# A decoder step in which VectorE turns the cached keys in 32x32 blocks, TensorE scores them by 32x32 block products, and the memory keys come first

## The reference, cut to what matters

```python
k_all = concatenate([pool_k[page_table].reshape(Bd, P, KV, 128), k_new], axis=1)   # cached pages, then the new key
s = einsum('bqkgd,blkd->bkgql', qg, k_all) * 128 ** -0.5                           # 8 samples x 12 heads x 2049
s = s + bias                     # layer 0: ALiBi and the mask of the chosen 256; layer 1: forgetting bias
p = softmax(s); o = einsum('bkgql,blkd->bqkgd', p, v_all)
sm = einsum('bqhd,bmhd->bhqm', qm, cache_mem_k) * 128 ** -0.5                       # 8 x 4 x 256 memory scores
```

## Time and profile before

| | before |
|---|---|
| time, three runs | 2242.54, 2244.25, 2245.08 us |
| profiled execution, first to last instruction | 2232.3 us |
| TensorE busy | 2170.8 us, 97% |
| VectorE busy | 661.5 us, 30% |
| ScalarE busy | 485.6 us, 22% |
| DMA, all queues | 647.34 MB, mean 290 GB/s |
| granted TensorE clock, mean | 0.990 |

### The profile page before, as it was taken

The page is one execution under the profiler, slowest core; times in us unless marked ns, Lnnn a source line. Parts: engine busy times, 40 slices in busy tenths (PEclk is TensorE's granted clock), DMA queues, the critical chain, the costliest instruction groups (busy, mean ns, idle before and its releaser), DMA issues.

```text
span 2232.3 us, 32324 instructions
## 1 busy us (share of the span) xinstructions
PE 2170.8 (97%) x12529; PEld 1346.5 (60%) x12529; DVE 661.5 (30%) x1225; ACT 485.6 (22%) x1106; POOL 4.3 (0%) x10
## 2 busy tenths in 40 slices
PE   8999999999999999999899999999999999999999
PEld 7778875678844435343488886645788444343534
DVE  0239961610662222212500010033115622222223
ACT  1221016520331001010310215643104211010112
POOL 0000000000000000000000000000000000000000
PEclk9999999999999999999999999999999999999999
DMA  9743548794359999999955457998642699999994
GB/s 274 233 149 115 198 152 259 214 344 150 114 228 425 420 429 413 428 420 422 380 164 161 144 188 245 356 348 305 243 145 107 248 426 425 427 427 429 424 428 192
DMA packets 213854, 647.34 MB, mean 290 GB/s; under 512 B 55400, under 2 KB 88953, under 8 KB 184161
## 3 DMA queue, kind: packets, MB, share of 16 engines
q1 hardware_dynamic: 180673, 637.39, 73.8%
q10 hardware_dynamic: 33056, 8.27, 1.9%
HBM read 639.62 MB, written 5.96 MB: 289 GB/s over the span
## 4 chain that ended last, share of the span: by engine, by line
PE 88%; DMA 9%; ACT 2%; DVE 1%; issue 1%; SPq 0%; ACTq 0%; DVEq 0%
PE bank L681 22%; PE bank L1379 14%; PE bank L1178 10%; PE bank L1426 9%; PE bank L1440 6%; DMA ring<-in_w_down 5%; PE bank L915 4%; DMA ring<-in_w_up 4%; PE bank L1352 4%; PE bank L925 2%; PE bank L1055 2%; PE bank L1036 1%; ACT arena L1528 1%; PE bank L1002 1%; PE bank L1262 1%; PE bank L970 1%
## 5 line engine op out<-in xcount | busy, mean ns | idle before, releaser
L1379 PE MATMUL bank<-ring,AT 128*64 128x512 f32 x2048 | 457.3, 596 | 11.5 <-DMA ring<-in_w_up 8.2
L1528 ACT ACTIVATE arena<-bank 128x512 f32<-128x512 f32 (+5 forms) x519 | 255.8, 540 | 811.5 <-PE bank L681 231.0
L681 PE MATMUL bank<-X,ring 128*128 128x264 f32 x1664 | 385.6, 389 | 6.2 <-ACT X L1778 6.2
L681 PEld LDWEIGHTS bank<-X,ring 128*128 128x128 f32 x1664 | 312.3, 191 | 64.2 <-issue 13.3
L1379 PEld LDWEIGHTS bank<-ring,AT 128*64 128x64 f32 x2048 | 142.4, 137 | 287.2 <-issue 272.4
L1426 PE MATMUL bank<-ring,arena 128*64 128x512 f32 x1024 | 224.3, 594 | 18.7 <-ACT arena L1528 13.8
L1178 PE MATMUL bank<-AT,ring 128*128 128x264 f32 x1024 | 232.6, 390 | 0.0
L2441 DVE TENSOR_TENSOR X<-bank,X 128x264 f32<-128x264 f32 x256 | 110.7, 432 | 361.6 <-PE bank L1440 359.6
L1178 PEld LDWEIGHTS bank<-AT,ring 128*128 128x128 f32 x1024 | 196.8, 193 | 34.1
L1426 PEld LDWEIGHTS bank<-ring,arena 128*64 128x64 f32 x1024 | 75.6, 137 | 157.2 <-issue 154.5
L1440 PE MATMUL bank<-arena 128*128 128x264 f32 x512 | 138.8, 402 | 0.0
(11 more groups left out here) (342 smaller groups left out, 1385.2 us busy)
## 6 DMA issues: line engine op xcount, KB each, us to landing
ring<-in_w_gate SPq DMA_DIRECT2D x64, 2048.0 KB, 16.8
ring<-in_w_up SPq DMA_DIRECT2D x48, 2048.0 KB, 15.5
ring<-in_w_down SPq DMA_DIRECT2D x48, 2048.0 KB, 12.9
ring<-in_w_o SPq DMA_DIRECT2D x16, 2048.0 KB, 12.1
ring<-in_w_up SPq DMA_DIRECT2D x32, 1024.0 KB, 7.6
ring<-in_w_down SPq DMA_DIRECT2D x32, 1024.0 KB, 15.8
ring<-in_cache_b_k SPq DMA_DIRECT2D x128, 256.0 KB, 4.3
ring<-in_cache_b_v SPq DMA_DIRECT2D x128, 256.0 KB, 4.8
```

The source lines that it names most:

```text
L681: mm = pe.matmul(B[4 * (g % 2) + f][:, 0:n_tok], u[:, c * 512 + f * P:c * 512 + (f + 1) * P], src[8 * half + c][:, 0:n_tok], start=(half = ...
L1379: mm = pe.matmul(B[bank][64 * s:64 * s + 64, :], M.xsT[:, at:at + 64], ring[slots[s][0]][:, c * FE:(c + 1) * FE], start=(half == 0 and c = ...
L1528: return act.activation(out, in_, ACT.Copy, scale=scale)
```

## The change

The cached keys are no longer turned by TensorE and copied by ScalarE. VectorE turns each `k` unit in place with one instruction (`turn_keys`), which transposes each 32x32 block by itself. Inside a block of 32 positions and 32 head numbers the numbers now lie along 32 partitions; the four blocks of positions of a page lie in the four partition quarters. So a product has 32 rows and 32 columns: `Qz` is built with each of the four quarters d of the query copied to all four partition quarters (`query_blocks` on TensorE, `pad_queries` on ScalarE), and partition quarter r writes its scores to bank r, summed over d and the key heads. In layer 0 a unit is now one sample with 16 pages and a product group holds 4 units; in layer 1 a unit is one sample with 8 pages and a group holds 2.

The memory units stand ahead of the cached units in the plan, in the scores and in the softmax; the four memory heads use four 32-column groups instead of two, in tiles of their own in `AT`. The new key's scores come from products on VectorE (`new_keys`) and one matmul. The spread mask is added by TensorE behind the last group (`cached_mask`), and `add_mask` is gone. The first half of `prompt_topk` stands behind the turning of the keys, the second half in the middle of the softmax of the cached scores.

```diff
-    u += [("k", k, 128 // n) for k in range(n)] + [("mk", k, 4) for k in range(2)]
+    u += [("mk", k, 4) for k in range(2)] + [("k", k, 128 // n) for k in range(n)]
...
+        def key_unit(layer, u):
+            if layer == 0:
+                return u, 0, PAGES
+            return 2 * (u // 4) + u % 2, 8 * (u // 2 % 2), PAGES // 2
...
+            def query_blocks(a, x):
+                if x == 4:
+                    pe.wait_ge(S("slab_copied"), cnt["slab"] - 1)
...
+                    for d in range(4):
+                        for r in range(4):
+                            mm = pe.matmul(B[4][32 * r:32 * r + 32, 96 * d:96 * d + 96], ident[:, 32 * d:32 * d + 32], new,
+                                           start=True, stop=True)
...
-                slab(layer, "mkv", 0, Ac, SEQ)
+                slab(layer, "mkv", 0, Ac, SEQ, lambda x: query_blocks(a, x))
+                pe.wait_ge(S("q_padded"), (8, 25)[layer])
...
+                def product(group):
+                    us = range(n_seq * group, n_seq * (group + 1))
+                    pe.wait_ge(S("keys_made"), key_base(layer) + us[-1] + 1)
...
+                    for kv in range(a.nk):
+                        for d in range(4):
+                            for u, tile in zip(us, tiles):
...
+                                for r in range(4):
+                                    rows = slice(32 * r, 32 * r + 32)
+                                    mm = pe.matmul(B[r][out, 32 * first:32 * (first + per)],
+                                                   a.Qz[kv // 2][rows, at:at + 32],
+                                                   tile[rows, :, kv * P + 32 * d:kv * P + 32 * d + 32],
...
+                                if kv == a.nk - 1 and d == 3:
+                                    leave(mm, layer, "k", u)
...
+                pe.wait_ge(S("natural_copied"), cnt["natural"])
...
+                pe.wait_ge(S("q_padded"), (9, 26)[layer])
...
+                    if b % 4 == 3:
+                        leave(mm, layer, "mk", b // 4)
+                mem_product(NB - 1).then_inc(S("km_scores"), 1)
+                for group in range(n_unit // n_seq):
+                    mm = product(group)
+                pe.wait_ge(S("keys_made"), (9, 26)[layer])
+                new = pe.matmul(B[6][:, 0:1], a.kp, cst("ones")[:, 0:1], start=True, stop=(layer == 1))
+                if layer == 0:
+                    new = cached_mask(a)
...
-                pe.wait_ge(S("s_norm"), 2 * layer + 1)
+                pe.wait_ge(S("s_norm"), 2 * layer + 2)
...
+            def turn_keys(layer, us):
+                for u in us:
+                    t = arrived(dve, layer, "k", u)
+                    dve.transpose(t[:, :], t[:, :]).then_inc(S("keys_made"), 1)
...
                 dve.tensor_reduce(nm[:, 0:1], S_, AX.X, ALU.max, negate=True).then_inc(S("s_max"), 1)
-                dve.wait_ge(S("s_exp"), 2 * layer + 1)
+                if layer == 0:
+                    prompt_topk(a, 1)
+                dve.wait_ge(S("s_exp"), 2 * layer + 2)
...
-                    prompt_topk(a)
-                    add_mask(a)
+                    turn_keys(layer, range(8))
+                    new_keys(layer, a)
+                    prompt_topk(a, 0)
```

More of the change, by code:

```diff
@@ L512, in _ @@
                     elif name == "k":
-                        n_seq = UNIT // (4 * W)
-                        q, j, half = k * n_seq // 16, k * n_seq // 4 % 4, k * n_seq % 4
-                        for b in range(n_seq):
-                            pages(full(layer, s), 4 * q + half + b, 4 * j, 4, ck,
-                                  lambda g: t[:, (4 * b + g - 4 * j) * W:(4 * b + g - 4 * j + 1) * W])
+                        b, first, per = key_unit(layer, k)
+                        pages(full(layer, s), b, first, per, ck, lambda g: t[:, (g - first) * W:(g - first + 1) * W])
                     elif name == "v":
@@ L943, in sample_scores @@
-                n_self = 4 * len(groups)
-                for m in range(n_self):
-                    turn(m)
-                    if m % 4 == 1 and m > 4:
-                        product(m // 4 - 1)
-                new_key()
-                product(len(groups) - 1).then_inc(S("k_scores"), 1)
-                def mem_product(b, hp, m):
-                    pe.wait_ge(S("ks_copied"), base + m + 1)
-                    for s in range(2):
-                        h = 2 * hp + s
-                        mm = pe.matmul(B[7][32 * s:32 * s + 32, 0:SEQ], a.Qmz[:, (h * NB + b) * 32:(h * NB + b + 1) * 32],
-                                       a.KTk[m % 6][:, SEQ * s:SEQ * (s + 1)],
-                                       start=(b == 0 and hp == 0), stop=(b == NB - 1 and hp == 1))
-                    return mm
@@ new lines, in cached_mask @@
+                def cached_mask(a):
+                    pe.wait_ge(S("mask_ready"), 1)
+                    m = a.S[0:NB, 0:PAST].rearrange("b (g r j) -> b g r j", r=4, j=32)
+                    for r in range(4):
+                        pe.matmul(B[r][:, :], cst("to12", NB), m[:, :, r, :], start=False, stop=True)
+                    return pe.matmul(B[6][:, 0:1], cst("to12", NB), a.S[0:NB, PAST:L1], start=False, stop=True)
+                pe.wait_ge(S("natural_copied"), cnt["natural"])
+                base = layer * KM_STEPS
@@ new lines, in mem_product @@
+                def mem_product(b):
+                    pe.wait_ge(S("km_copied"), base + 2 * b + 2)
+                    for h in range(HM):
+                        mm = pe.matmul(B[7][32 * h:32 * h + 32, 0:SEQ], a.Qmz[:, (h * NB + b) * 32:(h * NB + b + 1) * 32],
+                                       a.KTm[(2 * b + h // 2) % 4][:, SEQ * (h % 2):SEQ * (h % 2 + 1)],
+                                       start=(b == 0), stop=(b == NB - 1))
+                    return mm
+                pe.wait_ge(S("q_padded"), (9, 26)[layer])
@@ L2512, in _ @@
                     cached_gates(a)
+                    turn_keys(layer, range(16))
+                    new_keys(layer, a)
                 sample_softmax(layer, a)
```

201 lines of the change are left out of this document (84 added, 117 removed).

## The result

The changed kernel takes 2256.14 us (median of 4; 2253.99 to 2258.61) against 2243.53 before (4 runs beside it, 2242.54 to 2245.08). The ratio is 1.0063, 95% interval 1.0045 to 1.0082: 12.6 us slower by the medians, 14.1 by the ratio. 2258 was forecast, and slower.

The account below looks back on a forecast made before the run. TensorE was 88% of the chain of waits, barely slower than both supplies, SP's issues and DMA. Layer 0 +18.3 and layer 1 -4.7 gave +13.6 us, the median going from 2244.25 to 2258, range 2243 to 2290.

Parts of the forecast that it names:

- Issue pace and ring order in layer 0: Layer 0: memory units first push key issues back, 80 at 0.664 us ending at 377.3; rows turned 16.8 us later.
- Turning a unit on VectorE: Both layers: VectorE turns a 4096-column key unit in 4.6 us, from estimates of 2.6, 4.6 and 5.7.
- Rival B: Both layers: turning on VectorE is slow, 10 us a unit, layer 1's rows 47 us later; 2310 us; chance 6%.
- The block products: TensorE's scores of cached keys: a group takes 7.4 us plus 4.3 for the mask in layer 0, 8.0 in layer 1.
- rival A: Block products are slow: at twice the length layer 1's rows come 47 us later, layer 0 8 later; 2313 us; chance 12%.
- The top-k on the path: Layer 0's softmax on VectorE: the second half of the prompt's top-k takes 9.1 us and covers the exponential.
- The values' own floor: Layer 0: if VectorE's chain were free, the values alone would hold the shift near +11 us.
- The clock: TensorE at half clock after idle time: 2 us added in layer 0, 3 in layer 1.
- Layer 1: DMA paces the keys, TensorE's 30 us saving is lost waiting; rows -7.2 us, clock +3, memory softmax -0.5: -4.7.
- The median: Whole kernel: +18.3 in layer 0 and -4.7 in layer 1, +13.6 us, from 2244.25 to 2258.

Follow-up runs that it names:

- e5_act: On e1_topk: in layer 0 ScalarE, not SP, issues the second half of the pages of k5, k6 and k7; 2238.1 us, ratio 0.9980 to before.
- e4_noturn: Changed kernel with VectorE turning only the first 32 columns of every key unit (scores are others); 2263.9 us, ratio 1.0099 to before.
- e1_topk: Changed kernel with both halves of the prompt's top-k moved into VectorE's waits between layer 0's k0 and k3 turnings; 2248.8 us, ratio 1.0024 to before.
- e3_clock: Changed kernel with 44, 24 and 14 added products keeping TensorE busy in its waits; 2272.6 us, ratio 1.0136 to before.
- e9_clock: On e1_topk: 33, 9 and 9 added products keep TensorE busy in its waits; 2249.5 us, ratio 1.0027 to before.
- e2_half: Changed kernel loading only half the pages of every cached key unit, both layers (scores are others); 2225.2 us, ratio 0.9927 to before.

## Why the prediction was right, step by step

It was right in sign and in size, and in its mechanism for layer 0 and for the keys of layer 1. Several terms were off and made up for one another, so part of the closeness is luck. Set beside the steps of the trace it used:

- **Issue pace and ring order in layer 0.** Values' issues forecast from 377.3, measured 376.8; last unit turned at 384.0, measured 382.4. e5_act shows the cause. k3 was to be issued at 324.2; its first issue stands at 324.5.
- **Turning a unit on VectorE.** 4.6 us from bounds of 2.6 to 5.7; measured 4.45. e4_noturn: one turning, 4 us, is all that it costs in layer 0. Rival B is out, and with it the estimate of 10 us from the Trainium skill's "VectorE: DVE Perf Modes" ("The three transpose paths"). The Trainium skill's rule that the transpose keeps up one element per cycle per lane ("Vector Engine (DVE) Microarchitecture Reference", section 3.8) is in line with the trace, which has no cycles but 1.09 ns a column, as much as the reduction, which reads one element a column (1.12).
- **The block products.** This term was too small. A round of 16 blocks was taken at 0.93 us, so a group at 7.4; it takes 8.70 (1.09 a round), and 10.2 to 11.3 after a wait. In layer 1 8.0 stood for 7.4 of products and some 1.6 of gaps; against rival A the prediction had read off 32 records in 0.43 us that issuing is no limit, and these gaps are "issue". In layer 0 the forecast had VectorE come last (398.0) and TensorE before it (395.7); it was the other way round, 395.9 and 397.2. The two errors offset each other: the scores were read at 397.3, the rows turned at 413.5 (414.4).
- **The top-k on the path.** 9.1 us in place of an exponential of 2.2: e1_topk takes 6.5 from the rows.
- **The values' own floor, "near +11".** e1_topk's mix is at +11.0, with 1.6 us of waiting for transfers in its attention. In the prediction this stood as a remark; it turned out to be the second bound of layer 0, and three experiments ran into it.
- **The clock.** +2 in layer 0 and +3 in layer 1. The longer turnings are there (3.67 against 1.97), and e3_clock shows that the wait makes them; filling the waits won 2.6 us on the path of layer 0's rows in e9_clock, and nothing in the time. What the prediction did not count is larger: the clock loss in layer 1's attention and experts, 9.0 and 3.5 us before, 8.3 and 12.8 after, 6.8 to 23.2 and 3.7 to 13.2 in the other traces.
- **Layer 1.** Forecast -4.7; the first pair of traces said -5.6, all traces -3.5, the timings -3.9. The rows came at -4.7 to the projection in the first pair (-4.3 in all), not -7.2, for the last group took 9.7 instead of 8.0 and the memory keys began 1.2 late. Bytes as the pace of the keys: shown by e2_half, where the waits between groups vanish. Behind the rows it is TensorE at its granted clock.
- **The median.** 2258 against 2256.1. The sum was +18.3 - 4.7 = 13.6; the medians differ by 12.6. The traces do not add up to that: against the mean of before's two the changed kernel's has +15.6 in layer 0, -8.2 in layer 1's stage and +12.5 in the experts of both layers, of which the forecast had nothing, and its span is 2255.1 where 2245.9 was forecast. Both traces of before are of executions under its median, so the medians are the fair measure of the sum, and the traces that of its steps.

Open: why TensorE's clock in layer 1's attention and experts differs from one execution to another, whether the change has a part in that, and what the "issue" gaps in the block products are.

## What to carry to other kernels

When an engine waits for nothing, look one step behind it before taking its work away: here both supplies, issue pace in one layer and bytes in the other, stood close behind it, so 33 us of saved TensorE work in layer 1 bought about 4. In a ring, count for every unit who issues it, how many issues it takes and how long its slot is held; a cheap unit moved to the front pushes dear ones back, and a consumer that takes units in fours holds back even what comes after them. And of a stage with two nearly equal bounds, one trace tells neither: compare several kernels' milestones, or trace the old one again. Where the same code takes different times, read the granted clock of the stretch before blaming the transfers: an engine that is busy throughout can still be the one that is slower.

## What the runs showed of the hardware

- Row and column blocks of 32x32 do run side by side: 128 products of 512 columns (256 records, each 0.59 us long by the profile's modelled ends) in 8.70 us, so by that estimate some 17 records are under way at once.
- Products of 32x256 with their weight loads stop for 0.2 to 2 us after every 128 records of layer 1 in e2_half, where no transfer is awaited, and mostly so in the changed kernel. In the changed kernel such gaps come to 27.5 us over layer 1's 2048 records, and to 3.7 over the 512 of 32x512 in layer 0.
- After waits of 3.5 (e9_clock), 9.4 and 30.7 us TensorE worked at a lower granted clock, 0.60, 0.57 and 0.57 in the first 3.4 to 4.5 us; behind back-to-back 512-column products (e3_clock) it was 1.00. Being busy was not enough: in layer 1's attention, of small products and busy 99%, the mean was 0.81 to 0.94, and the same records took up to 1.9 times as long.
- Two queues issuing 128 KB pages moved 303 GB/s where one moved 199 in the same stretch (e5_act).
- An issue of a cached page costs ScalarE's queue 0.70 us (16.87 for 24), about what it costs SP's (0.63).
- STREAM_TRANSPOSE of 4096 fp32 columns takes 4.45 us, 1.09 ns a column, hardly more than a reduction (1.12).
